# Forgetting scores on two row tiles, their bias added by VectorE, in a new order

## What is computed

```
F = jnp.cumsum(log_f, axis=1).transpose(0, 2, 1)
...
s = jnp.einsum('bhqd,bhkd->bhqk', qi, kh)          # qi is scaled by 64 ** -0.5
s = s + Fi[..., None] - F[:, :, None, :]
s = jnp.where(key_pos[None, :] <= qpos[:, None], s, NEG)
p = jax.nn.softmax(s, axis=-1)
return jnp.einsum('bhqk,bhkd->bhqd', p, vh)
```

## Time and profile before

| what | us |
| --- | --- |
| median of 3 runs | 1972.53 |
| lowest and highest | 1971.71, 1975.39 |
| profiled execution, span from first to last instruction | 1970.0 |
| TensorE busy in it | 1925.6 |
| VectorE, ScalarE, GpSimd busy | 1198.0, 923.5, 945.3 |

### The profile page before, as it was taken

How to read it: one execution, slowest core, us unless ns; L and a number is a source line. 1 busy time by engine, 2 the same in 40 slices (tenths; PEclk the granted TensorE clock), 3 DMA queues, 4 the chain that set the end, 5 groups by cost and what they waited for, 6 DMA issues and landing times.

```text
span 1970.0 us, 28999 instructions
## 1 busy us (share of the span) xinstructions
PE 1925.6 (98%) x11395; PEld 1595.0 (81%) x11395; DVE 1198.0 (61%) x1932; ACT 923.5 (47%) x1747; POOL 945.3 (48%) x702
## 2 busy tenths in 40 slices
PE   6999999999999999999999999999999999999998
PEld 5878787888788878888888888888688777889986
DVE  6587979694566646664544440345765575876664
ACT  4555756564455544233434342344655454534442
POOL 1343323234534226564444444454474561788883
PEclk9999999999999999999999999999999999999999
DMA  8256353543321117664332334335122323233333
GB/s 310 76 168 191 110 182 117 182 145 105 107 62 55 43 56 285 226 227 158 96 107 86 107 85 148 99 115 187 55 74 81 82 55 115 85 98 97 89 121 138
DMA packets 92327, 242.48 MB, mean 123 GB/s; under 512 B 28192, under 2 KB 31392, under 8 KB 90784
## 3 DMA queue, kind: packets, MB, share of 16 engines
q1 hardware_dynamic: 89312, 232.24, 37.3%
q10 hardware_dynamic: 2880, 8.39, 1.1%
HBM read 223.14 MB, written 14.29 MB: 121 GB/s over the span
## 4 chain that ended last, share of the span: by engine, by line
PE 89%; DVE 3%; POOL 3%; ACT 2%; DMA 1%; issue 1%; SPq 0%; ACTq 0%; DVEq 0%
PE ps L1002 21%; PE ps L1003 20%; PE ps L1013 20%; PE ps L1372 3%; PE ps L1447 2%; PE ps L1434 2%; PE ps L1038 1%; PE ps L1037 1%; PE ps L1422 1%; PE ps L1349 1%; PE ps L1048 1%; PE ps L1509 1%; PE ps L1103 1%; PE ps L1110 1%; PE ps L1104 1%; POOL wlo L3069 1%
## 5 line engine op out<-in xcount | busy, mean ns | idle before, releaser
L3068 POOL TENSOR_TENSOR wlo<-raww,whi 128x512 fp32r<-128x512 f32 x217 | 303.6, 1399 | 668.3 <-ACT whi L1576 667.8
L1576 ACT CAST whi<-raww 128x1024 fp32r<-128x1024 f32 (+2 forms) x299 | 295.4, 995 | 197.3 <-PE ps L1013 134.4
L3069 POOL TENSOR_TENSOR wlo<-raww,whi 128x512 fp32r<-128x512 f32 x217 | 309.7, 1427 | 0.0
L1002 PE MATMUL ps<-hT_h,whi 128*128 128x512 f32 (+1 forms) x688 | 251.3, 374 | 2.4 <-DVE st L2480 1.7
L1003 PE MATMUL ps<-hT_l,whi 128*128 128x512 f32 (+1 forms) x688 | 244.6, 365 | 0.0
L1013 PE MATMUL ps<-hT_h,wlo 128*128 128x512 f32 (+1 forms) x688 | 152.4, 364 | 0.0
L1002 PEld LDWEIGHTS ps<-hT_h,whi 128*128 128x128 f32 x688 | 129.8, 189 | 27.3 <-issue 3.4
L1003 PEld LDWEIGHTS ps<-hT_l,whi 128*128 128x128 f32 x688 | 129.9, 189 | 21.9 <-issue 1.7
L1013 PEld LDWEIGHTS ps<-hT_h,wlo 128*128 128x128 f32 x688 | 119.2, 189 | 20.7 <-issue 0.5
L1002 PE MATMUL ps<-h_h,whi 128*128 128x512 f32 x336 | 130.7, 389 | 0.0
L1003 PE MATMUL ps<-h_l,whi 128*128 128x512 f32 x336 | 130.7, 389 | 0.0
(11 more groups left out here) (642 smaller groups left out, 4863.8 us busy)
## 6 DMA issues: line engine op xcount, KB each, us to landing
ec<-csd SPq DMA_DIRECT2D x32, 1024.0 KB, 8.2
raww<-in_w_up SPq DMA_DIRECT2D x44, 512.0 KB, 3.6
modr<-in_w_mod SPq DMA_DIRECT2D x32, 512.0 KB, 5.9
raww<-in_w_xbc SPq DMA_DIRECT2D x24, 512.0 KB, 3.8
raww<-in_w_gl SPq DMA_DIRECT2D x24, 512.0 KB, 3.9
raww<-in_w_z SPq DMA_DIRECT2D x16, 512.0 KB, 3.6
raww<-in_w_g SPq DMA_DIRECT2D x16, 512.0 KB, 3.6
raww<-in_w_os SPq DMA_DIRECT2D x16, 512.0 KB, 4.0
```

What stands on the lines that cost most here:

```text
L1002: e.matmul(o, whi[:, i, c], hi(k)[:, t0:t1], start=(k == 0), stop=False)
L1576: e.copy(o, x.rearrange("p (k c) -> p k c", c=64) if p == plan.first["dt", 0] else x).then_inc(*w_high.mark(("high", p)))
L3068: e.tensor_tensor(o[:, 0:512], x[:, 0:512], h[:, 0:512].bitcast(F32), ALU.subtract).then_inc(*p_wlow.mark(("first half", p)))
L3069: e.tensor_tensor(o[:, 512:1024], x[:, 512:1024], h[:, 512:1024].bitcast(F32), ALU.subtract).then_inc(*p_wlow.mark(("split", p), ("raw fre ...
```

## The change

Scores are made for a pair of heads at once. One ACT instruction evicts a product of two heads as it lies into `fhead` (128 partitions, 512 tokens). The F32 matmuls use 64 partitions each, one head on partitions 0 to 63 and the other on 64 to 127, in alternation and into two banks. There is no row of sums in them. The mask is added in two halves of 64 rows, one with a 64 x 128 slice of `eyes` (zeros and an identity) and 128 columns, one with 64 columns; so there are four mask matmuls for a block of a pair, where there were two.

The forget sums go from SBUF to DRAM (`fd`, 24 KB) once. SP waits until they have landed and reads each pair's 1024 sums back into all 128 partitions (`fbias`, 512 KB, two buffers). DVE's new pass adds `fbias` to the scores, takes the row's minimum of their negation and writes the scores to `Pf` (two instructions each: the pass and a read of the accumulator). The bank is then free. ACT's exponential reads and writes `Pf`.

The order of the second block is written out by hand (`second_block_steps`, and `LAST_MOVES` on top), in place of `fox_steps`, `memory_steps`, `s5_steps` and part of `AHEAD_OF`: scores of a pair, then products, then all its 20 transposes in a row. The first 20 steps of the powers stand before `fl`, on DVE between the last update of `X` and the forget logits; step `forget` stands before `s5load`, and the loads of `u` (24 DMAs) are in three parts.

```diff
 def second_block_steps():
...
+    o += scores(0) + [("fq", 7), ("fscored", 0), ("fqout", 7), ("fq", 2)] + turns(0) + [("fqout", 2)]
...
 LAST_MOVES = [
...
+    (('s5zero',), ('u', 4)), (('forget',), ('s5load',)), (('fin', 5), ('fin', 6)),
...
-        qk = sbuf("qk", [P, 2, 4, L], 114)
+        fhead = [sbuf(f"fhead{i}", [P, 2, L], 114 + 8 * i) for i in (0, 1)]
...
+        fbias = [sbuf(f"fbias{i}", [P, 2, L], kb) for i, kb in enumerate((118, 126))]
+        eyes, fmask = sbuf("eyes", [P, 192], 133.5, BF16), sbuf("fmask", [P, 192], 161.5, BF16)
...
+                    banks = [bank(("fscore", h, FGROUP[g][0]), OLDEST) for h in pair]
...
+                    for n in FGROUP[g]:
+                        a, Wd, c = (128 if n == 1 else 0), (n + 1) * 128, slice(n * 128, (n + 1) * 128)
+                        for h, b in zip(pair, banks):
+                            e.matmul(ps[:, b, a:a + Wd], fboth(p, 0)[fside(h), c], fboth(p, 1)[fside(h), 0:Wd], start=True, stop=False)
+                        for half, w in ((0, 128), (1, 64)):
+                            for h, b in zip(pair, banks):
+                                last = e.matmul(ps[:, b, a + Wd - w:a + Wd], eyes[fside(h), 64 - 64 * half:192 - 64 * half],
+                                                fmask[fside(h), 128 * half:128 * half + w], start=False, stop=(half == 1))
...
-                    for h in (0, 1):
-                        e.mul(fqk(2 * (m % 6) + h, i)[0:64, :], ps[64 * h:64 * h + 64, b, :], 1.0 if i else 0.125).then_inc(
-                            *a_moved.mark(*[("out of", (src, 0)), ("fq", m)] * h))
+                    e.mul(fboth(p, i), ps[:, b, :], 1.0 if i else 0.125).then_inc(*a_moved.mark(("out of", (src, 0)), ("fq", m)))
...
+                            e.tensor_tensor_reduce(out=frow(h % 2, n), in0=fscores(h, n), in1=fbias[p % 2][:, h % 2, 0:(n + 1) * 128],
+                                                   scale=-1.0, scalar=3.0e38, op0=ALU.add, op1=ALU.min, accum_out=sm[:, 1:2]).then_inc(
+                                *v_step.mark(("frow max", h, n), *drained))
...
+                    e.dma_start(A["fd"].rearrange("p a (h l) -> (p a h) l", l=L), ffs[:, 0, :]).then_inc(*f_out.mark(("forget sums kept",)))
+                    SP.wait_ge(at("forget sums kept"))
+                    for p in (0, 1):
+                        e.dma_start(fbias[p][:, :, :].rearrange("p h l -> p (h l)"), A["fd"][p].to_broadcast([P, 2 * L])).then_inc(
+                            *f_in[p].mark(("forget row", p)))
```

More of the change, by code:

```diff
@@ L259, in beside_window @@
     return out + sum((gate_steps(i) for i in range(9, 15)), [])
[L262 to L295, removed]
@@ L298, in memory_steps @@
[L298 to L316, removed]
@@ L319, in s5_steps @@
[L319 to L333, removed]
@@ L436, in order @@
         o[a], o[b] = o[b], o[a]
+    for step, other in LAST_MOVES:
+        o.remove(step)
+        o.insert(o.index(other), step)
     return o
@@ L489, in steps @@
     o += [("fin", 4), ("fin", 5)] + [("xturn", 0, c) for c in range(4)] + [("fin", 6), ("fin", 7), ("u", 3)] + [("xturn", 1, c) for c in range(4)]
-    o += [("fence", "two"), ("fl",), ("s5load",), ("forget",), ("u", 4), ("u", 5), ("fq", 0), ("s5zero",)] + [("s5u", m) for m in range(3)]
-    chain = [(SHARE["fq"], [("fqout", 0), ("fq", 6)]), (0.0, [("fqout", 6)])]
-    chain += tm_steps("w_fv", [0], 4, SHARE["fv"]) + [(SHARE["fq"], [("fq", 1)]), (0.0, [("fqout", 1)])] + fox_steps() + memory_steps()
-    o += merge(s5_steps(), chain)
-    o += [("yin",), ("gs", 0), ("gs", 1), ("fence", "glu")]
+    o += powers(0, 20) + [("fence", "two"), ("fl",), ("s5load",), ("forget",), ("u", 4), ("u", 5)] + second_block_steps()
+    o += [("gs", 0), ("gs", 1), ("fence", "glu")]
     parts = [[("fpair", k) for k in range(4)], [("fpair", 4), ("fpair", 5), ("mpair", 0), ("mpair", 1)],
@@ L1496, in tensor_program @@
                 elif k == "fscore":
-                    _, h, n = s
-                    if h == 0 and n == 0:
+                    _, p, g = s
+                    pair = (2 * p, 2 * p + 1)
+                    if p == 0 and g == 0:
                         ring_of_gemms[0] = OLDEST
-                    if n != 1:
-                        b = bank(s, OLDEST)
-                        PE.wait_ge(at("fq", h // 2))
-                        PE.wait_ge(at("fq", 6 + h // 2))
-                        PE.wait_ge(at("forget row", h))
-                        PE.wait_ge(at("rows of ones"))
-                    for i, a in {0: ((0, 0), (1, 128)), 1: (), 2: ((2, 0),), 3: ((3, 0),)}[n]:
-                        Wd = (i + 1) * 128
-                        e.matmul(ps[:, b, a:a + Wd], fqk(h, 0)[:, i * 128:(i + 1) * 128], fqk(h, 1)[:, 0:Wd], start=True, stop=False)
-                        e.matmul(ps[:, b, a + i * 128:a + Wd], maskb[:, 0, :], maskb[:, 2, :], start=False, stop=True).then_inc(
-                            *scores_done.mark(("fscores", h, i)))
+                    banks = [bank(("fscore", h, FGROUP[g][0]), OLDEST) for h in pair]
+                    PE.wait_ge(at("fq", p))
+                    PE.wait_ge(at("fq", 6 + p))
+                    PE.wait_ge(at("mask halves"))
+                    for n in FGROUP[g]:
[6 more added lines that the diff above has]
+                                                fmask[fside(h), 128 * half:128 * half + w], start=False, stop=(half == 1))
+                                if half:
+                                    last.then_inc(*scores_done.mark(("fscores", h, n)))
                 elif k == "fpt":
@@ L3107, in pool_program @@
                     after_last()
[L3108 removed]
+                    e.memset(eyes[:, :], 0.0).then_inc(*p_made.mark(("eyes clear",)))
                     after_last()
[L3110 to L3112 removed]
                 elif k == "root" or k == "rms" and s[1] not in ("y", "mem", "in", "x1", "x2"):
```

167 lines of the change are left out of this document (108 added, 59 removed), and 9 rows, old and new, of tables (AHEAD_OF, LAST_MOVES).

## The result

The changed kernel takes 1976.24 us (median of 20 runs, 1973.29 to 1978.46), the kernel before 1972.67 us (20 runs, 1971.41 to 1975.4). The ratio is 1.0016, with a 95% interval of 1.001 to 1.0022: about 3 us slower, where the prediction was 1961.5 (1956 to 1970). The profiled execution after took 1975.4 us with a span of 1974.0, 4.0 over the span before.

A forecast was written before the change was run, and what follows sets the result against it. It took the columns TensorE streams as the bound: span 1970.0 - 12.4 (scores) + 1.2 (waits) = 1958.8 us, and with 2.5 up to the runs' median 1961.3, stated as 1961.5; range 1956 to 1970.

The forecast's parts named there:

- What bounds the kernel: Stage around the forgetting attention: bound by the columns TensorE streams; other engines' work counts only where TensorE waits.
- The scores: TensorE's score matmuls: two heads overlap on row tiles, 18.8 us for 31.2, a gain of 12.4 (11.2 to 14.2).
- The rivals of partial and no overlap: Score tiles share the array only partly (about 1969.7 us, chance 0.12) or not at all (about 1978.5, chance 0.08).
- The estimate of 1.54: Speedup of two row tiles in the scores, under partial overlap: F32 18.7 us in place of 13.8, time about 1964.
- VectorE's pass and ScalarE's eviction: Softmax pass 0.685 us plus accumulator read 0.20; paired evictions save ScalarE 14 us over 24 products; all hidden under matmuls.
- The powers, "0 to 3 us later": First 20 power steps on VectorE ahead of the forget logits take 16 to 20 us; forget sums 0 to 3 later.
- SP, "so that is hidden": SP's queue: the forget sums' write and reads put the weights back 4 to 8 us, hidden before TensorE's need at 1372.
- The first rival: First pair late: braw delays VectorE's first extremum, ScalarE's queue follows; price 4 to 6 us, about 1966.5, chance 0.20.
- Waits, "2.0 (0 to 6)" for the softmax: TensorE's waits for a pair's softmax between its scores and transposes: an allowance of 2.0 us (0 to 6).
- two of 1.0 and 1.4 for the transposes: Transposes of pairs 0 and 1 wait for banks that ScalarE evicts late: 1.0 and 1.4 us, 2.4 in the sum.
- Forecast waits +1.2: TensorE's net waits: -3.2 for two old waits gone, +2.4 for transposes, +2.0 for the softmax, +1.2 us.

The follow-up runs named there:

- e2: Changed kernel with VectorE's power steps 14 to 19 behind the forget chain instead of ahead of it; 1968.6 us.
- e1: Changed kernel with, on SP's queue alone, the forget sums' write and reads behind the fqk weights and the loads of braw, cc and dd ahead; 1970.98 us.
- e7: Changed kernel with the loads of braw, cc and dd ahead of the forget step again, the sums still ahead of the fqk weights; 1972.59 us.
- e3: Changed kernel with the fifth turning of B moved later and the third memory gate product ahead of the memory value product; 1972.06 us.
- e9: Changed kernel with the fifth forget gate product behind the fourth state group's taps, and VectorE's scan ahead of the copy of the taps; 1972.09 us.
- e6: e2 with 20 and 12 added mask matmuls, whose results are overwritten, in the waits for BA and PTm; 1965.6 us.
- e11: e10 with, in addition, e1's edit of SP's queue; 1961.44 us, ratio 0.9943 to the kernel before.
- e8: Changed kernel with the fourth group's turning of B and third state product ahead of the second memory query product, its drive ahead of the third; 1979.55 us.
- e5: Changed kernel with the edits of e8 and e2 and e3's move of the third memory gate product; 1972.44 us.
- e10: Changed kernel with the edits of e9 and e2 and e3's move of the third memory gate product; 1964.13 us.
- e4: Changed kernel with each row block's score matmul and masks written head by head instead of alternating between the pair's heads; 1975.73 us.
- e12: e11 with pairs 2 to 5 written as all score calls of one head, then all of the other; 1969.32 us.

## Why the prediction was wrong, step by step

- *What bounds the kernel*: right as read, but only for the kernel before. "VectorE's and ScalarE's work counts only where TensorE comes to wait for it" was then checked for the softmax, not for the chains that the scores had covered.
- *The scores*: right in the mechanism, and in the number by two errors of 0.9 that cancel, which is luck. One head's 2.60 stood for all twelve, 31.2 us, and they take 30.3; 18.8 was forecast for after and 17.9 measured (a pair was put at 3.0 and takes 2.94, and the pairs entered twice 0.12 more each, for the 0.8 put at the entries). The rivals of partial and no overlap fell. The estimate of 1.54 fell too: it was worked out from the Trainium skill (TensorE: Matmul & The Clock Gate, Measured speedup vs the span model) and would have made the F32 part 18.7, where all of the scores took 17.9, masks included. (Its "about 1964" sets the 18.7 against the F32 part of the sum, about 15.6; from the 13.8 named beside it, it would be about 1966.)
- *VectorE's pass and ScalarE's eviction*: the pass right, the eviction's saving put at double. There are twelve products, not 24: 24 instructions of 0.59 (L1902) became 12 of 0.60 (L1897), 7 us less and not 14. Nothing in the sum hung on it. The pass takes 0.679 at 512 (0.685 was taken), the accumulator read 0.081 (0.20 was taken, 0 to 0.3).
- *The powers, "0 to 3 us later"*: mis-sized. The sums leave 8.0 us later: the chain starts 7.0 later and takes 1.0 longer. 1.7 of it is the stretch at 1298, which is not of the change. The powers took 1323.4 to 1346.05, 22.6 us for the 16 to 20 forecast: a few of the small operations were held for over a microsecond (last section). e2 shows what the 8.0 cost.
- *SP, "so that is hidden"*: **the first step that failed.** The weights were put at 4 to 8 us later and compared with TensorE's need of them at 1372. The first went out at 1364.65, where the trace before has it at 1353.76, so 10.9 later, and was there for the rounding at 1371.42, 6.8 after its issue and not the 3.7 of the earlier trace rows. And what TensorE needed first was not the weights but two banks whose evictions queue behind their rounding on ScalarE. The first rival named ScalarE's order and about the right price (4 to 6 us; e1 4.8 by the rest, 5.9 by the medians), but put it on `braw`; e7 shows that the wait stands without it.
- *Waits, "2.0 (0 to 6)" for the softmax, two of 1.0 and 1.4 for the transposes*: the transposes' waits are there, 1.4 in all for 2.4. The softmax took nothing. **The second step that failed** is that nothing was allowed for the chain of the state groups: the work that filled it before was what the change moved ahead of it. e3 and e9 show the chain. The `gm 2` move was not priced at all: 2.4 of wait and 1.6 of half rate, of which e3, with a new wait of 1.6 behind it, shows 2.3.
- *The clock*: no term stood for it. The trace before holds 1.00 through waits of 1.9 and 1.3 us; three longer ones gave half rate, 5.5 us in all; e6 gets some 3 us of it back.

Forecast waits +1.2; measured +9.3 of idle and 5.5 of half rate behind it. That difference, 13.6, is the miss of the span (1974.0 for 1958.8), with the 1.7 at 1298. With the three places mended, e11 reaches the forecast's number, though by moves that the change did not make.

## What to carry to other kernels

Work taken from the busiest engine is also the cover of every chain that runs beside it: before counting the gain, list for each chain (a table on GpSimd, a state update, a queue of loads) the time between the step that starts it and the one that needs it, before and after, with only the remaining work in between. Follow a late transfer to every instruction that queues behind its first reader, not only to the engine that uses the data. And price a wait on a busy TensorE above its length: here the three waits of 9.9 us cost 5.5 more at half rate, though not every wait is followed by it.

## What the runs showed of the hardware

- *Waits and the clock.* Waits of TensorE of 2.4, 3.6 and 3.9 us (after), 3.6 (e3) and 5.3 (e8) were each followed by matmuls at a granted 0.50, and so was one of 1.96 in e5 (0.58 and 0.57 in the two stretches of 2 us behind it); after those of 1.9 and 1.3 before and 1.6 in e11 it stayed at 1.00. But it also stayed at 1.00 after the same wait of 2.4 for `PTm` in e9 and in e8. TensorE in e9:
```profile
1620.95 1.12 PE L1546 MATMUL ps<-PTm,mv 128*128 128x512 f32 x2 [2.37 <-ACT PTm L1978]
...
1627.38 0.60 PE L1539 MATMUL ps<-cst,Pq 128*128 128x128 f32 x4
```
That is 6.43 us from the end of the wait to the transposes, 6.44 in e8, and 8.07 after (1622.61 to 1630.68), with the same instructions: the price of this half rate, 1.6 us, and the sign that a wait's length does not settle whether it comes. The stretch at 1298 follows sixteen matmuls of one column that take 1.8 us, with no wait there. Executions of e2, e5, e9, e10 and the changed kernel have it, those of the kernel before, e1, e3, e4, e6, e7, e8, e11 and e12 have not, with the same instructions up to there; those of e9 and e10 have another at 514, behind waits of 0.7 and 0.6. Why one has it and the other not stays open.
- *VectorE beside GpSimd.* The timelines of VectorE and GpSimd after, in the powers:
```profile
1330.41 2.41 DVE L2280 COPY pk__66<-pk__66 128x24 f32<-128x24 f32 x2
...
1338.04 1.25 DVE L2229 TENSOR_TENSOR z<-z,ztmp 128x24 f32<-128x24 f32 x1
...
1331.50 1.29 POOL L3074 TENSOR_TENSOR wlo<-raww,whi 128x512 fp32r<-128x512 f32 x1
...
1337.93 1.29 POOL L3073 TENSOR_TENSOR wlo<-raww,whi 128x512 fp32r<-128x512 f32 x1 [5.15 <-ACT whi L1571]
```
Copies and products of this size take 0.18 to 0.22; these end at 1332.82 and 1339.29, with GpSimd's instructions (1332.79, 1339.22). The Trainium skill (SBUF — State Buffer, SBUF: two separate sides) says that the two engines share a pair of ports as an exclusive lock, held for a whole instruction; the trace agrees, and the price is set by the other engine's instruction, over a microsecond for a 0.2 us step.
- *Row tiles.* The Trainium skill (TensorE: Matmul & The Clock Gate, The mechanism) has matmuls start and end strictly in program order. e4's records differ: the second head's F32 records start ahead of the first head's masks, which stand ahead of them in the program; within one head they keep its order; the measurement decides.
